# The low parts of the feed-forward weight units made by VectorE in place of GpSimd

## The chip, the cores and the metric

One Trainium2 chip, one of its cores. The metric is the device time of one execution in microseconds (us). Before the change it is 3954.25 us, the median of 3 runs (3954.13 to 3955.24). Lower is better.

## The reference, cut to what matters

Two model blocks run one after the other, on 512 tokens of width 1024. The first has two layers (a gated linear attention, a state space scan, memory attention); the change doesn't touch it. The second puts 16 meta tokens ahead of the 512 and has two layers, each a mixer and then a feed-forward block:

```
D_MODEL = 1024; D_FF = 4 * D_MODEL; N_META = 16; DEPTH = 2

def sq_relu_mlp(h, w1, w2):
    return jnp.square(jax.nn.relu(h @ w1)) @ w2

for i in range(DEPTH):
    g = norm_g[i]
    hn = rmsnorm(h, g[0])
    m = rwkv_pool_mixer(hn, ...) if i % 2 == 0 else diff_attn_mixer(hn, ...)
    h = h + rmsnorm(m, g[1])
    f = sq_relu_mlp(rmsnorm(h, g[2]), mlp_w1[i], mlp_w2[i])
    h = h + rmsnorm(f, g[3])
return h[:, N_META:]
```

## The kernel before, in words

**Weights.** All weights are one stream of units of 128 x 1024 floats. SyncE loads unit u into slot u mod 4 of `ring` (L2696 to L2709) once TensorE has begun unit u-2. The products of the feed-forward blocks are made at better than single-pass precision: a value is written as a high part, rounded to the format that TensorE takes in one pass, and a low part, the rest. For a unit of weights, ScalarE copies `ring` into one of two `high` buffers (`make_high`, L306 to L311), and GpSimd writes `ring` minus `high` into `ring_r` (`make_low`, L299 to L304) and counts the semaphore `unit_lo` up. TensorE waits for `unit_lo` before the first matmul of a unit (L184), and then issues for each of eight 128-row pieces k of the unit three products: high by high (L225), high weights by low activations (L228), low weights by high activations (L230). `make_high` of unit u+1 waits until TensorE has begun unit u (L310), so the parts are made one unit ahead.

**A feed-forward block** (`mlp`, L2590 to L2640) is four products, each a `Gemm`: in0, out0, in1, out1. An in-product makes 16 tiles of 128 features, from one unit each (8 k-pieces). An out-product makes 8 tiles from two units each. So there are 32 + 32 units in a block and 128 in both. In the first block (layer 0) a tile is 528 tokens wide, in two halves of 264; in the second (layer 1) 512. The f tiles of in0 are used up by out0, those of in1 by out1, which adds out0's sum.

**The engines' order.** Every engine runs the stages of the list `stages` in order, and within one its own loop; nothing is reordered on an engine, so a wait holds what stands behind it. Around a block:

- `Rms` (L399) norms the block's input. Its DVE part (L497 to L519) takes the reciprocal of the root (L505), and then for eight tiles k writes the normed tile (L513) and, two tiles later, the tile's low part `h_r` (L518), after ScalarE's high part `h_hi` (L478). Each of the eight low parts counts a semaphore.
- `rms.feed(g)` (L524 to L527) ties the first tile of in0 to these: `high` of its first unit is made in `Rms.scalar` (L475), before the normed tiles are there, and TensorE waits in the first tile for the low part of each k alone (L221, L222), not for all eight.
- ScalarE evacuates each in-tile with a relu (L2605). DVE's stage `Squares` (L2610 to L2627) then squares the tile (L2623), copies its high part `f_hi` (L2625) and makes its low part `f_r` (L2627).
- An out-product needs all 16 tiles' parts (L2638, L2639): TensorE and ScalarE wait for the last `f_r`. Its tiles are evacuated by ScalarE and VectorE in turn in out0 (L2243, L2246), by VectorE alone in out1 (L2608), whose squares for the next norm ScalarE makes (L441).
- The first matmul of any product waits until all tiles of the one before are evacuated (L201 to L203).

The core of the norm's DVE loop, for the order in which DVE's work stands:

```
507        for k in range(self.n + 2):
512            if k < self.n:
513                b.nc.vector.scalar_tensor_tensor(
514                    out=self.out(k), in0=self.view(self.x(k)), scalar=self.w(k),
516            if self.hi and k >= 2:
517                dve.wait_ge(b.out_hi, at["parts"] + k - 1)
518                b.nc.vector.tensor_tensor(self.lo(k - 2), self.out(k - 2), self.hi(k - 2),
```

Of the kernel before, what the change touches and what calls it, by code (L numbers as in the profile page):

```python
# [50 lines left out]
class Chain:  # L51


    def __init__(self, eng, sem):
        self.eng, self.sem, self.n = eng, sem, 0
# [29 lines left out]
class Stage:  # L85
# [8 lines left out]
    def vector(self, dve):  # L94
        pass

    def gpsimd(self, pool):
        pass


class Gemm(Stage):
# [13 lines left out]
    def __init__(self, b, name, kind, x, kt, outs, ranges, store, engines, needs, tiles=None, before=None,  # L115
                 high=None, x_hi=None, after=None, ready=None):
        self.ready = ready
        self.fed = False
        self.squared_by = None
        self.beside = False  # L120
        self.after = after
        self.b, self.name, self.kind, self.x, self.kt = b, name, kind, x, kt
        self.ranges, self.store, self.engines, self.needs = ranges, store, engines, needs
        self.tiles, self.before = tiles, before
        if kind == "fm":
            self.per_out = kt // 8
            self.slots = 4 if len(ranges) == 1 else 2
            self.body_outs = self.slots
            while self.body_outs * self.per_out % RING:
                self.body_outs += self.slots  # L130
            if outs < self.body_outs or outs % self.body_outs:
                self.body_outs = outs
            self.body_units = self.body_outs * self.per_out
            self.iters = outs // self.body_outs
            self.pars = [o % 2 for o in range(self.body_outs)]
        else:
            self.body_units = kt // 2
            self.body_outs = len(tiles)
            self.slots = len(tiles)
            self.iters = outs  # L140
            self.pars = [i % 2 for i in range(len(tiles))]
        self.unit0 = b.units
        self.full0 = list(b.full)
        self.body_par = [self.pars.count(0), self.pars.count(1)]
        self.peel = min(self.full0) == 0 or self.iters == 1 or before is not None or high is not None
        self.high, self.x_hi, self.split0 = high, x_hi, b.splits
        if high is not None:
            assert self.body_units % 2 == 0, name
            b.splits += self.body_units * self.iters
        b.units += self.body_units * self.iters  # L150
        b.full = [f + self.iters * n for f, n in zip(b.full, self.body_par)]
        self.done = list(b.full)
        if self.iters > 1:
            assert self.body_units % RING == 0, name
# [141 lines left out]
                it, j = divmod(u + 1, self.body_units)  # L296
                self.make_low(pool, j, it)

    def make_low(self, pool, j, it):  # L299

        b, slot = self.b, (self.unit0 + j) % RING
        pool.wait_ge(b.unit_hi, self.split0 + j + 1 + it * self.body_units)
        b.nc.gpsimd.tensor_tensor(b.ring_r[:, slot, :], b.ring[:, slot, :], self.high[:, j % 2, :],  # L303
                                  ALU.subtract).then_inc(b.unit_lo, 1)  # L304

    def make_high(self, act, j, it):  # L306
# [77 lines left out]
        evacuate(last, self.iters - 1, False)  # L384

    def gpsimd(self, pool):
        if self.high is None or self.beside:
            return

        def body(it):  # L390
            for j in range(self.body_units):
                self.make_low(pool, j, it)
        self.loop(pool, body)

    def vector(self, dve):
        self.evacuate(dve, "dve")


class Rms(Stage):  # L399
# [1757 lines left out]
def build(nc, a, out):  # L2157

    with ExitStack() as ctx:
        b = Board(nc, ctx)  # L2160
# [70 lines left out]
        def view(off, *shape):  # L2231
            n = int(np.prod(shape))
            ap = arena[:, off:off + n]
            if len(shape) == 1:
                return ap
            names = "abc"[:len(shape)]
            return ap.rearrange(f"p ({' '.join(names)}) -> p {' '.join(names)}",
                                **{c: s for c, s in zip(names[1:], shape[1:])})
# [89 lines left out]
        g = stages[-1]  # L2328
# [25 lines left out]
        g = stages[-1]  # L2354
# [10 lines left out]
        g = stages[-1]  # L2365
# [29 lines left out]
        g = stages[-1]  # L2395
# [24 lines left out]
        g = stages[-1]  # L2420
# [42 lines left out]
        g = stages[-1]  # L2463
# [61 lines left out]
        def norm_g(layer, i):  # L2525
            return lambda k: b.col("norm_g_2", (4 * layer + i) * 8 + k)
# [7 lines left out]
        def post(layer, i, g, kept=False):  # L2534

            if kept:
                rms = Rms(b, h3, KD, FULL, D, EPS, norm_g(layer, i), h3, [0], [], done(g), onto=x1, each=g.tile,
                          added=True)
            else:
                rms = Rms(b, h2, KD, HALVES, D, EPS, norm_g(layer, i), h2, [0, 1], [], done(g), onto=x2, each=g.tile,  # L2540
                          added=True)
            rms.follow(g)
            stages.append(rms)
            return rms
# [6 lines left out]
        def pre(layer, i, before, kept=False):  # L2551
            if kept:
                rms = Rms(b, x1, KD, FULL, D, EPS, norm_g(layer, i), h3, [2], [], hi=h3_hi, lo=h3_lo, each=before.tile)
            else:
                rms = Rms(b, x2, KD, HALVES, D, EPS, norm_g(layer, i), h2, [2, 3], [], hi=h_hi, lo=h2_lo,
                          each=before.tile)
            stages.append(rms)
            return rms
# [6 lines left out]
        def keep3(to):  # L2565
            return lambda which, m, parts, o: copy(which, to(m), parts[0])
# [23 lines left out]
        def mlp(layer, rms, kept=False):  # L2590

            at = META if kept else 0
            ranges = FULL if kept else HALVES
            f, f_lo, f_hi = b.f, b.f_lo, b.f_hi
            first = view(2 * F_TILES * L2, KD, L2)
            rms = pre(layer, 2, rms, kept)

            def filled(o, parts):
                return parts[0] if kept else b.ps[:, 2 * (o % 2):2 * (o % 2) + 2, 0:L2 // 2]

            def shaped(ap):
                return ap[:, at:] if kept else ap.rearrange("p (r t) -> p r t", r=2)

            def relu(which, m, parts, o):
                return nc.scalar.activation(shaped(f[:, m, :]), filled(o, parts), ACT.Relu)  # L2605

            def both_halves(which, m, parts, o):
                return nc.vector.tensor_tensor(shaped(b.h[:, m, :]), shaped(first[:, m, :]), filled(o, parts), ALU.add)  # L2608

            class Squares(Stage):  # L2610


                def __init__(self, g, base):
                    self.g, self.base = g, base

                def vector(self, dve):
                    with dve.Fori(0, 4) as it:
                        for o in range(4):
                            par, n = self.g.count(o, it)
                            done = it * 12 + (self.base + 3 * o)  # L2620
                            dve.wait_ge(b.stored[par], n)
                            t, hi, lo = (z[:, it * 4 + o, at:] for z in (f, f_hi, f_lo))
                            nc.vector.tensor_tensor(t, t, t, ALU.mult).then_inc(mlp_parts, 1)  # L2623
                            dve.wait_ge(mlp_parts, done + 1)
                            nc.vector.tensor_copy(hi, t).then_inc(mlp_parts, 1)  # L2625
                            dve.wait_ge(mlp_parts, done + 2)
                            nc.vector.tensor_tensor(lo, t, hi, ALU.subtract).then_inc(mlp_parts, 1)  # L2627

            for half in range(2):
                base = 48 * (2 * layer + half)  # L2630
                g = gemm(f"mlp{layer}_in{half}", h3_lo if kept else h2_lo, KD, 16, relu, A, [rms.ready], high,
                         h3_hi if kept else h_hi, ranges)
                if half == 0:
                    rms.feed(g)
                stages.append(Squares(g, base))
                whole = keep3(lambda m: first[:, m, META:]) if kept else keep2(lambda m: first[:, m, :])
                store, engines = (both_halves, V) if half else (whole, BOTH)
                g2 = gemm(f"mlp{layer}_out{half}", lambda k: f_lo[:, k, at:], 16, KD, store, engines,  # L2638
                          [(mlp_parts, base + 48)], high, lambda k: f_hi[:, k, at:], ranges)  # L2639
            return post(layer, 3, g2, kept)  # L2640

        rms = mlp(0, rms)


# [38 lines left out]
        for h in range(8):  # L2683
            o = lambda k, h=h: m3.o[:, h, :]
# [86 lines left out]
```

## Time and profile before

| | before |
|---|---|
| median of 3 runs | 3954.25 us (3954.13 to 3955.24) |
| the profiled execution's own time | 3962.14 us |
| its span | 3960.6 us |
| mean granted clock of TensorE | 0.879 |
| TensorE matmul busy | 3284.0 us, 83% |
| VectorE (DVE) busy | 1408.0 us, 36% |
| GpSimd (POOL) busy | 992.2 us, 25% |
| ScalarE (ACT) busy | 852.8 us, 22% |

The profile is of one execution. Its own time lies 7.9 us above the median of the runs without a profile. The span is from its first to its last instruction. The engine names in its rows are PE (TensorE's matmuls), PEld (its weight loads), DVE, ACT, POOL and SP (SyncE); L and a number is a line of the kernel. The granted clock is 1.0 where TensorE is given its 2.4 GHz and 0.5 at 1.2 GHz. An average over the whole span mixes stages with different limits, so what a change in one stage is worth has to be read in that stage. The first feed-forward block fills about 2557 to 2950 us of the span, the second about 3560 to 3940 us.

### The profile page before, as it was taken

What the parts mean: (1) busy time and instruction counts of PE and PEld (TensorE: products, weight loads), DVE (VectorE), ACT (ScalarE), POOL (GpSimd) and SP (SyncE); (2) the same over time, 40 slices, a digit from 0 to 9 for tenths busy, and PEclk for the clock granted to TensorE, in tenths of its full rate; (3) what the DMA queues carried; (4) which work ended last, traced back from release to release, by engine and by line L of the source; (5) the groups of instructions that cost most, each with busy time, mean ns of one, the idle gap of its engine ahead of it and who ended that gap; (6) DMA issues with size and microseconds to landing.
All of it is one profiled execution on the core that took longest, in us unless ns stands there. A gap on an engine that the chain in (4) does not pass through costs nothing.

```text
span 3960.6 us, 42750 instructions
## 1 busy us (share of the span) xinstructions
PE 3284.0 (83%) x16346; PEld 2473.8 (62%) x16346; DVE 1408.0 (36%) x2281; ACT 852.8 (22%) x1405; POOL 992.2 (25%) x691
## 2 busy tenths in 40 slices
PE   7997976698579699998895886899998855579997
PEld 4444745486466477446694775699988633337776
DVE  4663023501017512003326644350522243546052
ACT  2112222122012222001224111222222122222221
POOL 0220400243122276004340000043433400004443
PEclk9998976799879799999997996899999955589999
DMA  5991200023862168222220000122222100012222
GB/s 160 258 259 55 92 25 0 22 96 104 153 219 97 53 187 233 75 76 72 79 86 6 1 1 6 48 85 86 85 75 82 54 0 0 0 48 82 93 85 80
DMA packets 113984, 328.66 MB, mean 83 GB/s; under 512 B 35744, under 2 KB 36384, under 8 KB 113456
## 3 DMA queue, kind: packets, MB, share of 16 engines
q1 hardware_dynamic: 59040, 212.89, 16.9%
q0 software_dynamic: 32592, 101.46, 9.7%
q10 hardware_dynamic: 22208, 12.26, 1.2%
q8 instruction: 106, 1.74, 0.2%
q14 instruction: 38, 0.31, 0.0%
HBM read 290.48 MB, written 36.04 MB: 82 GB/s over the span
## 4 chain that ended last, share of the span: by engine, by line
PE 65%; DVE 18%; issue 5%; DMA 5%; POOL 4%; ACT 3%; DVEq 0%; ACTq 0%; POOLq 0%
PE ps L225 12%; PE ps L228 11%; PE ps L230 11%; PE ps L235 9%; DMA arena<-d_q 3%; DVE inv L505 2%; POOL ring_r L303 2%; PE ps L1918 2%; DVE h L513 2%; PE ps L1947 1%; PE ps L493 1%; PE ps L251 1%; PE ps L255 1%; DMA arena<-d_pb 1%; PE ps L254 1%
## 5 line engine op out<-in xcount | busy, mean ns | idle before, releaser
L303 POOL TENSOR_TENSOR ring_r<-ring,high 128x1024 fp32r<-128x1024 f32 x290 | 738.2, 2546 | 2107.2 <-ACT high L311 2106.8
L225 PE MATMUL ps<-h_hi,high 128*128 128x264 f32 (+1 forms) x1760 | 569.4, 335 | 73.7 <-DVE h_r L518 41.1
L228 PE MATMUL ps<-h_r,high 128*128 128x264 f32 (+1 forms) x1760 | 563.9, 332 | 0.0
L230 PE MATMUL ps<-h_hi,ring_r 128*128 128x264 f32 (+1 forms) x1760 | 496.8, 331 | 0.0
L311 ACT ACTIVATE high<-ring 128x1024 fp32r<-128x1024 f32 x290 | 305.9, 1055 | 601.3 <-PE ps L225 408.2
L225 PEld LDWEIGHTS ps<-h_hi,high 128*128 128x128 f32 x1760 | 336.5, 191 | 118.6 <-issue 71.3
L228 PEld LDWEIGHTS ps<-h_r,high 128*128 128x128 f32 x1760 | 337.9, 192 | 29.3
L235 PE MATMUL ps<-arena,ring 128*128 128x512 f32 (+1 forms) x896 | 337.5, 540 | 22.5 <-DVE arena L1759 10.0
L230 PEld LDWEIGHTS ps<-h_hi,ring_r 128*128 128x128 f32 x1760 | 300.8, 191 | 31.3
L235 PEld LDWEIGHTS ps<-arena,ring 128*128 128x128 f32 x896 | 172.5, 193 | 186.7 <-issue 158.6
L225 PE MATMUL ps<-f_hi,high 128*128 128x264 f32 (+1 forms) x768 | 241.3, 327 | 25.7 <-POOL ring_r L303 25.7
L228 PE MATMUL ps<-f_r,high 128*128 128x264 f32 (+1 forms) x768 | 239.9, 325 | 0.0
L235 PE MATMUL ps<-h,ring 128*128 128x512 f32 x512 | 220.3, 592 | 2.3 <-ACT arena L2243 2.3
L2246 DVE COPY arena<-ps 128x512 f32<-128x512 f32 (+4 forms) x32 | 21.2, 662 | 559.9 <-PE ps L230 284.5
L230 PE MATMUL ps<-f_hi,ring_r 128*128 128x264 f32 (+1 forms) x768 | 207.9, 325 | 0.0
L225 PE MATMUL ps<-z_hi,high 128*128 128x512 f32 x384 | 158.3, 412 | 37.3 <-POOL ring_r L303 36.3
L235 PEld LDWEIGHTS ps<-h,ring 128*128 128x128 f32 x512 | 97.1, 190 | 125.5 <-issue 125.5
L225 PEld LDWEIGHTS ps<-f_hi,high 128*128 128x128 f32 x768 | 147.8, 192 | 38.5 <-issue 26.9
L2627 DVE TENSOR_TENSOR f_r<-f,f_hi x64 | 157.4, 2460 | 2.2
L2243 ACT ACTIVATE arena<-ps 128x512 f32<-128x512 f32 (+6 forms) x104 | 59.7, 576 | 451.4 <-PE ps L230 256.4
L228 PE MATMUL ps<-z_lo,high 128*128 128x512 f32 x384 | 156.1, 407 | 0.0
L228 PEld LDWEIGHTS ps<-f_r,high 128*128 128x128 f32 x768 | 148.0, 193 | 11.7
(381 smaller groups left out, 4879.4 us busy)
## 6 DMA issues: line engine op xcount, KB each, us to landing
ring<-in_units SPq DMA_DIRECT2D x402, 512.0 KB, 3.5
d_ca<-arena POOLq DMA_DIRECT2D x16, 640.0 KB, 5.9
arena<-d_ca POOLq DMA_DIRECT2D x16, 640.0 KB, 5.0
arena<-in_s_bk POOLq DMA_DIRECT2D x16, 512.0 KB, 9.5
arena<-d_q POOLq DMA_DIRECT2D x32, 256.0 KB, 12.0
d_pb<-arena POOLq DMA_DIRECT2D x16, 512.0 KB, 7.2
arena<-d_pb POOLq DMA_DIRECT2D x16, 512.0 KB, 6.0
arena<-d_ca POOLq DMA_DIRECT2D x16, 512.0 KB, 6.7
```

The source lines that it names most:

```text
L225: part = mm(acc, hi[:, cols], self.x_hi(k)[:, t0:t0 + tn], start=(k == 0), stop=False)
L228: mm(acc, hi[:, cols], self.x(k)[:, t0:t0 + tn], start=False, stop=False)
L230: ins = mm(acc, w[:, cols], self.x_hi(k)[:, t0:t0 + tn], start=False, stop=(k == self.kt - 1))
L235: ins = mm(acc, w[:, k % 8 * P:(k % 8 + 1) * P], self.x(k)[:, t0:t0 + tn], start=(k == 0), stop=(k == self.kt - 1))
L251: part = mm(out, self.x_hi(k)[:, tok], hi, start=(k == 0), stop=False)
L303: b.nc.gpsimd.tensor_tensor(b.ring_r[:, slot, :], b.ring[:, slot, :], self.high[:, j % 2, :], ALU.subtract).then_inc(b.unit_lo, 1)
L311: b.nc.scalar.activation(self.high[:, j % 2, :], b.ring[:, u % RING, :], ACT.Copy).then_inc(b.unit_hi, 1)
L505: b.nc.vector.reciprocal(b.inv[:, 0:self.tokens], b.root[:, 0:self.tokens]).then_inc(b.inverted, 1)
L513: b.nc.vector.scalar_tensor_tensor(out=self.out(k), in0=self.view(self.x(k)), scalar=self.w(k), in1=self.view(b.inv[:, 0:self.tokens]), op ...
L1918: ins = mm(b.ps[0:nt, 2 * (n % 2) + c, 0:min(nk, 512)], q, k[:, 0:min(nk, 512)], start=True, stop=True)
L2243: return nc.scalar.activation(to, ps, ACT.Copy, scale=1.0 if scale is None else scale)
L2627: nc.vector.tensor_tensor(lo, t, hi, ALU.subtract).then_inc(mlp_parts, 1)
```

## The change

In both feed-forward blocks, and there alone, `make_low` is issued on VectorE. GpSimd has no instruction left in these eight products. In the in-products the stage `Squares` makes unit 0's low part first, and then, for each tile o, the low part of unit o+1 ahead of the squaring of tile o. Its loop of four passes over four tiles is written out. In the out-products `Gemm.vector` does the same around the evacuations that are VectorE's.

```
+        self.low_by = "pool"
...
+    def low_unit(self, dve, u):
+
+        if u < self.body_units * self.iters:
+            it, j = divmod(u, self.body_units)
+            self.make_low(dve, j, it)
+
+    def make_low(self, eng, j, it):
...
-        pool.wait_ge(b.unit_hi, self.split0 + j + 1 + it * self.body_units)
-        b.nc.gpsimd.tensor_tensor(b.ring_r[:, slot, :], b.ring[:, slot, :], self.high[:, j % 2, :],
+        eng.wait_ge(b.unit_hi, self.split0 + j + 1 + it * self.body_units)
+        which = b.nc.gpsimd if self.low_by == "pool" else b.nc.vector
+        which.tensor_tensor(b.ring_r[:, slot, :], b.ring[:, slot, :], self.high[:, j % 2, :],
                                   ALU.subtract).then_inc(b.unit_lo, 1)
...
     def gpsimd(self, pool):
-        if self.high is None or self.beside:
+        if self.high is None or self.beside or self.low_by != "pool":
             return
...
     def vector(self, dve):
-        self.evacuate(dve, "dve")
+        if self.low_by != "dve":
+            self.evacuate(dve, "dve")
+            return
+        b = self.b
+        self.low_unit(dve, 0)
+        for m in range(self.body_outs * self.iters):
+            for u in range(m * self.per_out + 1, (m + 1) * self.per_out + 1):
+                self.low_unit(dve, u)
+            it, o = divmod(m, self.body_outs)
+            if self.engines[self.pars[o]] == "dve":
+                par, n = self.count(o, it)
+                dve.wait_ge(b.filled[par], n)
+                self.store("dve", m, self.bank(o), o).then_inc(b.stored[par], 1)
+                if self.squared_by and m >= 2:
+                    self.squared_by.add(dve, m - 1)
...
                 def vector(self, dve):
-                    with dve.Fori(0, 4) as it:
+                    self.g.low_unit(dve, 0)
+                    for it in range(4):
                         for o in range(4):
+                            self.g.low_unit(dve, it * 4 + o + 1)
                             par, n = self.g.count(o, it)
...
+                g.low_by = "dve in Squares"
                 stages.append(Squares(g, base))
...
+                g2.low_by = "dve"
```

Lines of the changed kernel are 22 to 24 higher than those above: its L311 is L303, L540 is L518, L535 is L513, L2647, L2649 and L2651 are L2623, L2625 and L2627, and L2268 is L2246. Two places show the new order.

VectorE (DVE) at the start of in0 of layer 0, before: the last rows of the norm, then the first passes of `Squares`. `h_r` is the low part of a normed tile, `out_hi` the semaphore of its high part.

```order
L513 SCALAR_TENSOR_TENSOR h<-x,cols,inv 128x528
L518 TENSOR_TENSOR h_r<-h,h_hi 128x528 [waits out_hi] x3
L2617 UNCONDITIONAL_BRANCH
L2617 ISA
L2623 ISA [waits stored_even]
L2623 TENSOR_TENSOR f<-f 128x528
```

The same place in the changed kernel:

```order
L535 SCALAR_TENSOR_TENSOR h<-x,cols,inv 128x528
L540 TENSOR_TENSOR h_r<-h,h_hi 128x528 [waits out_hi] x3
L311 TENSOR_TENSOR ring_r<-ring,high 128x1024 [waits unit_hi] x2
L2647 TENSOR_TENSOR f<-f 128x528 [waits stored_even]
L2649 CAST f_hi<-f 128x528 [waits mlp_parts]
L2651 TENSOR_TENSOR f_r<-f,f_hi 128x528 [waits mlp_parts]
L311 TENSOR_TENSOR ring_r<-ring,high 128x1024 [waits unit_hi]
L2647 TENSOR_TENSOR f<-f 128x528 [waits stored_odd]
```

The low parts of units 0 and 1 now stand on VectorE behind the last low part of the norm; before, GpSimd had nothing else in its queue at this place.

VectorE from the last evacuations of out0 into in1 of layer 0, in the changed kernel (before, the rows of L2246 and of `Squares` stood here alone):

```order
L2268 COPY arena<-ps 128x528 [waits filled_odd]
L311 TENSOR_TENSOR ring_r<-ring,high 128x1024 [waits unit_hi] x3
L2268 COPY arena<-ps 128x528 [waits filled_odd]
L311 TENSOR_TENSOR ring_r<-ring,high 128x1024 [waits unit_hi] x2
L2647 TENSOR_TENSOR f<-f 128x528 [waits stored_even]
```

The low part of in1's first unit is the first of the two behind the last evacuation.

## Rows read from the trace of the kernel before

**Rows 1.** The page, part 1: busy us, share of the span, instructions.
```profile
PE 3284.0 (83%) x16346; PEld 2473.8 (62%) x16346; DVE 1408.0 (36%) x2281; ACT 852.8 (22%) x1405; POOL 992.2 (25%) x691
```
**Rows 2.** The page, part 4: the chain that ended last, by line.
```profile
PE ps L225 12%; PE ps L228 11%; PE ps L230 11%; PE ps L235 9%; DMA arena<-d_q 3%; DVE inv L505 2%; POOL ring_r L303 2%; PE ps L1918 2%; DVE h L513 2%; PE ps L1947 1%; PE ps L493 1%; PE ps L251 1%; PE ps L255 1%; DMA arena<-d_pb 1%; PE ps L254 1%
```
**Rows 3.** Timeline, layer 0's in0 begins: start us, us, instruction [idle before <-releaser].
```profile
2551.99 2.34 POOL L303 TENSOR_TENSOR ring_r<-ring,high 128x1024 fp32r<-128x1024 f32 x1 [123.55 <-ACT high L311]
2557.44 0.56 PE L225 MATMUL ps<-h_hi,high 128*128 128x264 f32 x1 [7.36 <-DVE h_r L518]
2563.08 1.94 DVE L518 TENSOR_TENSOR h_r<-h,h_hi 128x528 fp32r<-128x528 f32 x3
2567.31 0.39 PE L225 MATMUL ps<-h_hi,high 128*128 128x264 f32 x1 [1.02 <-POOL ring_r L303]
```
**Rows 4.** Timeline at the beginning of layer 1's in0.
```profile
3566.23 1.89 DVE L518 TENSOR_TENSOR h_r<-h,h_hi 128x512 fp32r<-128x512 f32 x3
3570.43 0.50 PE L225 MATMUL ps<-h_hi,high 128*128 128x512 f32 x1 [1.11 <-POOL ring_r L303]
```
**Rows 5.** Groups by line on DVE: count | busy us, mean ns | idle.
```profile
L1663 DVE TENSOR_TENSOR arena<-ps,memn 128x1024 f32<-128x1024 f32 x8 | 9.8, 1225 | 15.0 <-PE ps L1575 15.0
```
**Rows 6.** Timeline at three of the four in-to-out places, with two second units.
```profile
2658.11 1.06 ACT L311 ACTIVATE high<-ring 128x1024 fp32r<-128x1024 f32 x1 [2.20 <-DVE f_r L2627]
2659.25 2.34 POOL L303 TENSOR_TENSOR ring_r<-ring,high 128x1024 fp32r<-128x1024 f32 x1 [11.24 <-ACT high L311]
2661.73 0.56 PE L225 MATMUL ps<-f_hi,high 128*128 128x264 f32 x1 [6.46 <-POOL ring_r L303]
2670.49 1.06 ACT L311 ACTIVATE high<-ring 128x1024 fp32r<-128x1024 f32 x1 [7.04 <-PE ps L225]
...
2859.44 0.56 PE L225 MATMUL ps<-f_hi,high 128*128 128x264 f32 x1 [6.46 <-POOL ring_r L303]
...
3660.52 0.77 PE L225 MATMUL ps<-f_hi,high 128*128 128x512 f32 x1 [6.41 <-POOL ring_r L303]
3668.20 1.06 ACT L311 ACTIVATE high<-ring 128x1024 fp32r<-128x1024 f32 x1 [5.76 <-PE ps L225]
```
**Rows 7.** Timeline: steady tiles of in0, layer 0 and layer 1.
```profile
2602.79 0.61 ACT L2605 ACTIVATE f<-ps 128x528 f32 x1 [4.29 <-PE ps L230]
2603.56 0.71 DVE L2623 TENSOR_TENSOR f<-f  x1 [1.75 <-ACT f L2605]
2604.43 2.65 POOL L303 TENSOR_TENSOR ring_r<-ring,high 128x1024 fp32r<-128x1024 f32 x1 [3.19 <-ACT high L311]
2604.86 2.79 DVE L2627 TENSOR_TENSOR f_r<-f,f_hi  x1
2608.64 0.61 ACT L2605 ACTIVATE f<-ps 128x528 f32 x1 [4.29 <-PE ps L230]
...
3576.30 0.60 ACT L2605 ACTIVATE f<-ps 128x512 f32<-128x512 f32 x1 [4.21 <-PE ps L230]
3577.08 0.69 DVE L2623 TENSOR_TENSOR f<-f  x1 [4.87 <-ACT f L2605]
3581.86 0.60 ACT L2605 ACTIVATE f<-ps 128x512 f32<-128x512 f32 x1 [4.01 <-PE ps L230]
```
**Rows 8.** Timeline: the f_r of in0's second-last tile, layer 0.
```profile
2651.63 0.71 DVE L2627 TENSOR_TENSOR f_r<-f,f_hi  x1
```
**Rows 9.** Timeline from out0 to in1 of layer 0.
```profile
2758.25 0.71 DVE L2246 COPY arena<-ps 128x528 f32 x1 [22.69 <-PE ps L230]
2759.21 0.36 PE L225 MATMUL ps<-h_hi,high 128*128 128x264 f32 x1 [1.14 <-DVE arena L2246]
```
**Rows 10.** Windows: length; busy of PE, PEld, DVE, ACT, POOL; granted clock; DMA.
```profile
2655.50:2660.00 4.50, 0.00 (x0) 0.00 (x0) 1.85 (x3) 1.47 (x2) 0.75 (x1) 1.00 0.00 0
2855.00:2859.40 4.40, 0.00 (x0) 0.00 (x0) 0.76 (x2) 1.06 (x1) 2.34 (x1) 0.50 0.00 0
3533.40:3535.40 2.00, 0.00 (x0) 0.00 (x0) 0.69 (x1) 1.13 (x2) 0.00 (x0) 1.00 0.00 0
```

More of the change, by code:

```diff
@@ L297, in out_gpsimd @@
                 self.make_low(pool, j, it)
-    def make_low(self, pool, j, it):
+    def low_unit(self, dve, u):
[3 more added lines that the diff above has]
+    def make_low(self, eng, j, it):
         b, slot = self.b, (self.unit0 + j) % RING
-        pool.wait_ge(b.unit_hi, self.split0 + j + 1 + it * self.body_units)
-        b.nc.gpsimd.tensor_tensor(b.ring_r[:, slot, :], b.ring[:, slot, :], self.high[:, j % 2, :],
+        eng.wait_ge(b.unit_hi, self.split0 + j + 1 + it * self.body_units)
+        which = b.nc.gpsimd if self.low_by == "pool" else b.nc.vector
+        which.tensor_tensor(b.ring_r[:, slot, :], b.ring[:, slot, :], self.high[:, j % 2, :],
                                   ALU.subtract).then_inc(b.unit_lo, 1)
```

## The prediction

> **What bounds the kernel now.** The page's busy shares come first [rows 1]: TensorE is busy for 83% of the span, VectorE for 36%, GpSimd for 25%. The chain that ended last [rows 2] says the same by line: the split products L225, L228 and L230 lead it, and GpSimd's low part L303 has 2%. So of GpSimd's work only what lies in a gap of TensorE can be on the path, and the question goes to the timelines of the two feed-forward blocks. Three kinds of place are there.
>
> In a steady tile TensorE never waits. In layer 0 one relu starts at 2602.79 and the next at 2608.64 [rows 7], so a unit takes 5.85 us; in layer 1 it is 3576.30 to 3581.86, 5.56 us. GpSimd's 2.65 us lie inside. What GpSimd does to VectorE there is visible too: f_r takes 2.79 us while a GpSimd low part runs [rows 7] and 0.71 us where none does [rows 8].
>
> Where an in-product ends and an out-product begins, TensorE stands still for 6.46 us, released by GpSimd [rows 6]: squares, `high` at 2658.11, low part at 2659.25 for 2.34 us, first matmul at 2661.73. There are four such places, two in each layer.
>
> Where a norm feeds in0, GpSimd makes the first low part at 2551.99, long before it is wanted. TensorE begins the tile at 2557.44, released by the first `h_r`, and works beside the norm's remaining seven [rows 3]. The last of these ends at 2563.08 + 1.94 = 2565.02, and unit 1 begins at 2567.31. Layer 1 is alike: 3568.12 and 3570.43 [rows 4].
>
> **What the change does, part by part.** The changed price is that of one low part on VectorE. No row has this form. The nearest is a VectorE subtraction or product over the same 128x1024 elements with one operand in PSUM, 1.225 us [rows 5]; f_r, scaled from 528 elements and its 0.71 us to 1024, would give at most 1.38. I take 1.22, since its row has the same number of elements. GpSimd's 2.34 is the other end; at that price nothing would be gained where a low part is exposed.
>
> *In to out, four times.* The last squares, `high`, the low part and the first matmul still follow one another. 2.34 becomes 1.22, a gain of 1.12 each: **-4.5 us**. At 1.38 it is -3.8.
>
> *Start of in0, twice.* The order of VectorE's work has the first low part behind all eight `h_r`, and TensorE waits for it before its first matmul. The tile that ran beside the norm now starts after it. Layer 0: 2565.02 + 1.22 + 0.14 (0.14 is what passed from the end of the low part at 2661.59 to the matmul at 2661.73 [rows 6]) = 2566.4. The tile then takes a warm 5.85 us and what the clock costs. TensorE's first matmul takes 0.56 us after the norm and 0.39 us ten microseconds later [rows 3], so it starts on the lower clock. What a whole unit pays for that is seen after the in-to-out gap: 2661.73 to the next unit's `high` at 2670.49 is 8.76 us, less about 0.07 of latency and 5.85, so 2.85 more; in layer 1, 3660.52 to 3668.20, less 0.07 and 5.56, 2.05 more [rows 6]. I take 2.5, between the two, for either layer. Unit 1 can then begin at 2566.4 + 5.85 + 2.5 = 2574.7, where it began at 2567.31: 7.4 us later. Its own low part is ready by then, since `high` follows the first matmul at once and has the whole tile. Layer 1: 3568.12 + 1.36 + 5.56 + 2.5 = 3577.5 for 3570.43, 7.1 us. Together **+14.5 us**. If the clock cost nothing it would be +9.5, with 2.85 in both +15.2.
>
> *Out0 to in1, twice.* The evacuation of out0's last tile starts at 2758.25 and ends at 2758.96, and TensorE starts at 2759.21, released by it [rows 9]. The low part was ready; now it stands behind this evacuation on VectorE: +1.22 each, **+2.4 us**. TensorE's gap grows from 1.14 to 2.36 us.
>
> *The steady tiles, at nothing.* For tile o VectorE does the low part of unit o+1 and then tile o's squares, and what can be late is the low part that stands behind these squares. Layer 0: f_r starts at 2604.86 and, with GpSimd idle, ends at 2605.57 [rows 7, 8]; low part until 2606.8, TensorE released at 2606.9, wanted at about 2608.4, just ahead of the next relu. Spare: 1.5 us. Layer 1: squares from 3577.08, f_r 1.30 later as in layer 0, low part done at 3577.08 + 1.30 + 0.69 + 1.22 = 3580.3, released at 3580.4, wanted at 3581.6. Spare: 1.2 us. In the out-products VectorE's only other work is an evacuation or a sum of 0.7 us every second unit. `high` is still made one unit ahead and waits for nothing of VectorE's. The same holds for the DMA queue of SyncE, which waits for TensorE alone; GpSimd's queue only loses instructions. The loop written out costs VectorE no time that TensorE sees with over 1 us of spare.
>
> Here a rule bears. The Trainium skill (SBUF — State Buffer, Who interferes with whom) says that a VectorE instruction with two SBUF inputs and a GpSimd one that reads SBUF take turns on a shared read port, and that the loser stands still for the other's whole length. The rows agree: f_r ends 0.57 us after GpSimd's low part (2607.65 and 2607.08). By the rule f_r is short once GpSimd has left, which is what rows 8 show already; without it f_r could stay long, and that is the third rival.
>
> Another rule speaks for the change. The Trainium skill (GPSIMD Engine Reference, Engine selection) puts two-input elementwise work on VectorE, GpSimd being about twice as slow. The rows agree on the factor (2.34 against 1.225), but counted for all 128 low parts it would be 143 us, of which the sum above lets the path see 4.5.
>
> **Sum.** -4.5 + 14.5 + 2.4 = +12.4 us. On the profiled execution's own 3962.14 us that is 3974.5; that execution lies 7.9 us above the median of the runs, and the same difference on the median, 3954.25, gives **3966.7 us**.
>
> **Rivals.**
>
> *The clock stays up from in to out (the other side: not slower).* TensorE's gap there shrinks from 6.46 to 5.3 us. If the granted clock no longer fell in it, each of the four out-products would save the 2.5 us of its first unit as well: 12.4 - 10 = +2.4, 3956.6 us. It decides on whether the fall comes later than 5.3 us after the last matmul. For it: in the first of these gaps the clock is still full until 2660.00 [rows 10], 4.7 us after the last matmul (2661.73 - 6.46 = 2655.27 [rows 6]). Against: in the second of them, which begins at 2859.44 - 6.46 = 2852.98 [rows 6], it is at half from 2855.00 on [rows 10], and it has to stay up four times. Chance 0.08.
>
> *The clock falls before in1.* The gap of 2.36 us is longer than the 2.0 us without a matmul from 3533.40 to 3535.40, through which the clock stayed full [rows 10], and longer than the 2.0 us after which it had fallen in the gap just named. If it falls in both layers, 2 x 2.5: +17.4, 3971.7 us; in one, 3969.2. Chance 0.15.
>
> *VectorE becomes the bound of the in-products.* If f_r stayed at 2.79 us, or the low part took over 2.4, the low part would come late in each steady tile: in layer 0 2604.86 + 2.79 + 1.36 = 2609.0 for 2608.4, 0.6 us; in layer 1 0.9 us by the same count. 30 tiles of each, +45: 4012 us. Rows 8 speak against it. Chance 0.02.
>
> That it comes out faster for a reason that I don't see has 0.03. The forecast keeps 0.72.
>
> **How the numbers follow.** About 0.2%, 7.9 us, is what a measurement of this kernel can tell from no change: above 3962.2 is slower, below 3946.3 faster. The forecast's own range is 3962 to 3970 (from the in0 starts at almost no clock cost to the upper ends of all terms); it lies above the bound but for its low end, and so do the second rival and the third. I count 0.1 of the forecast's 0.72 as within the bound: slower 0.62 + 0.15 + 0.02 = 0.79, same 0.08 + 0.1 = 0.18, faster 0.03. The range, 3958 to 3973, reaches down to halfway to the first rival and up over the second with both layers and a low part at 1.38.
>
> **What would show it.** Right: at in0 in the changed profile TensorE idles for some 16 us with its first L225 released by the low part on DVE, about 1.4 us after the last `h_r`; relu to relu stays 5.85 and 5.56 us; the four in-to-out gaps are about 5.3 us; the gap before in1 is 2.3 to 2.4 us; f_r takes 0.7 us in all tiles; the low part on DVE takes 1.22 us. Wrong: waits of TensorE on the low part inside an in-product, a first unit of an out-product that starts with matmuls at the full clock, a low part much longer than 1.22 us, or a first tile of in0 that still overlaps the norm.

## The result, and the profile after

The change makes the kernel slower by a little: 3959.95 us, the median of 17 runs (3949.74 to 3971.6), against 3951.06 us for the kernel before (17 runs, 3937.59 to 3960.89). The ratio is 1.0027 with a 95% interval of 1.0014 to 1.0039, so +10.7 us, between +5.5 and +15.4; the two medians lie 8.9 us apart. The forecast was +12.4 us, and 3966.7 us on a median of before that more runs put 3.2 us lower (3951.06 for 3954.25).

The page of the kernel after, part 1, answers to [rows 1]:

```profile
span 3958.4 us, 42302 instructions
PE 3276.7 (83%) x16346; PEld 2470.5 (62%) x16346; DVE 1438.9 (36%) x2409; ACT 852.7 (22%) x1405; POOL 673.0 (17%) x563
```

and these are the two groups of the low part, of part 5 (count | busy us, mean ns | idle before):

```profile
L311 POOL TENSOR_TENSOR ring_r<-ring,high 128x1024 fp32r<-128x1024 f32 x162 | 417.4, 2577 | 1147.2 <-ACT high L319 1147.1
L311 DVE TENSOR_TENSOR ring_r<-ring,high 128x1024 fp32r<-128x1024 f32 x128 | 156.5, 1223 | 195.9 <-ACT high L319 195.9
```

128 low parts went from GpSimd to VectorE at 1.223 us each. GpSimd lost 319 us of work, VectorE gained 31 (157 for the low parts, less what f_r no longer loses). Neither number is in the kernel's time.

The profiled span of after is 2.2 us *shorter* than that of before, although the runs say slower. A pair of profiles doesn't settle a difference of this size as a whole; it does when read stage by stage. These are the reciprocals (L505 before, L527 after) ahead of in0 and behind out1, in the timelines of VectorE. Before:

```profile
2551.06 3.45 DVE L505 RECIPROCAL inv<-root 128x528 f32<-128x528 f32 x1 [2.86 <-ACT root L472]
2960.28 3.45 DVE L505 RECIPROCAL inv<-root 128x528 f32<-128x528 f32 x1 [2.20 <-ACT root L472]
...
3943.13 3.35 DVE L505 RECIPROCAL inv<-root 128x512 f32<-128x512 f32 x1 [2.00 <-ACT root L472]
```

After:

```profile
2542.49 3.45 DVE L527 RECIPROCAL inv<-root 128x528 f32<-128x528 f32 x1 [2.86 <-ACT root L494]
2956.49 3.45 DVE L527 RECIPROCAL inv<-root 128x528 f32<-128x528 f32 x1 [2.20 <-ACT root L494]
...
3548.57 3.35 DVE L527 RECIPROCAL inv<-root 128x512 f32<-128x512 f32 x1 [2.65 <-ACT root L494]
...
3941.36 3.35 DVE L527 RECIPROCAL inv<-root 128x512 f32<-128x512 f32 x1 [2.00 <-ACT root L494]
```

The stages ahead of the first block, which the change doesn't touch, took 8.57 us less in this execution, those between the blocks 2.2 less. The block of layer 0 went from 409.22 to 414.00 us, that of layer 1 from 388.60 (its reciprocal before started at 3554.53) to 392.79: **+8.97 us** in the two. This count, from reciprocal to reciprocal, is used for all runs below. From run to run it still holds the chance of how the granted clock falls and comes back around TensorE's gaps. In the six kernels here that have an in-to-out gap of 5.0 to 5.1 us, one execution of each, the first units of the four out-products (from the first matmul to the third `high`) add up to 30.9 to 34.4 us. So some 3 us between two kernels can be this alone, and smaller differences are read by place.

Where the 8.97 us come from, by places. The start of layer 0's in0, which answers to [rows 3] (timelines of VectorE and TensorE, after):

```profile
2554.51 1.94 DVE L540 TENSOR_TENSOR h_r<-h,h_hi 128x528 fp32r<-128x528 f32 x3
2556.37 1.22 DVE L311 TENSOR_TENSOR ring_r<-ring,high 128x1024 fp32r<-128x1024 f32 x1
2557.88 0.56 PE L226 MATMUL ps<-h_hi,high 128*128 128x264 f32 x1 [16.36 <-DVE ring_r L311]
```

TensorE stands idle for 16.36 us where it stood for 7.36, and its first matmul is released by the low part behind the last `h_r`. From in to out, and from out0 to in1, which answer to [rows 6] and [rows 9]:

```profile
2657.71 1.23 DVE L311 TENSOR_TENSOR ring_r<-ring,high 128x1024 fp32r<-128x1024 f32 x1 [1.12 <-ACT high L319]
2659.09 0.56 PE L226 MATMUL ps<-f_hi,high 128*128 128x264 f32 x1 [5.09 <-DVE ring_r L311]
2666.72 1.06 ACT L319 ACTIVATE high<-ring 128x1024 fp32r<-128x1024 f32 x1 [5.92 <-PE ps L226]
...
2754.34 0.71 DVE L2268 COPY arena<-ps 128x528 f32<-128x528 f32 x1 [8.78 <-PE ps L231]
2754.96 1.22 DVE L311 TENSOR_TENSOR ring_r<-ring,high 128x1024 fp32r<-128x1024 f32 x1
2756.32 0.36 PE L226 MATMUL ps<-h_hi,high 128*128 128x264 f32 x1 [2.02 <-DVE ring_r L311]
```

| place | before | after | measured | forecast |
|---|---|---|---|---|
| in0, layer 0: reciprocal to tile 1's relu | 22.40 | 29.69 | +7.29 | +7.4 |
| in0, layer 1: the same | 21.77 | 27.76 | +5.99 | +7.1 |
| in to out, the four gaps | 6.46, 6.46, 6.41, 6.42 | 5.09, 5.09, 5.04, 5.04 | -5.5 | -4.5 |
| the four first units of the out-products, from the first matmul to the third `high` | 8.76, 8.88, 7.68, 7.86 | 7.63, 7.84, 7.59, 7.87 | -2.3 | 0 |
| out0 to in1, the two gaps | 1.14, 0.99 | 2.02, 2.00 | +1.9 | +2.4 |
| in1's first unit, layer 0, to its relu | 6.11 | 7.63 | +1.5 | 0 |
| sum | | | +8.9 | +12.4 |

The steady tiles did not change: relu follows relu after 5.85 us in layer 0 and 5.55 to 5.56 us in layer 1, before and after.

### The profile page after: what moved, and what is told of

Read it like the earlier page. It is cut to its first block, busy times and chain, and to the rows that moved or that the text cites. A ratio compares the mean times of both kernels' runs of the same rounds, so it can differ in the third digit from the quotient of the medians.

```text
span 3958.4 us, 42302 instructions
## 1 busy us (share of the span) xinstructions
PE 3276.7 (83%) x16346; PEld 2470.5 (62%) x16346; DVE 1438.9 (36%) x2409; ACT 852.7 (22%) x1405; POOL 673.0 (17%) x563
## 4 chain that ended last, share of the span: by engine, by line
PE 71%; DVE 16%; POOL 4%; issue 4%; ACT 3%; DMA 2%; ACTq 0%; DVEq 0%; POOLq 0%
PE ps L236 15%; PE ps L226 11%; PE ps L229 11%; PE ps L231 11%; DVE inv L527 2%; POOL ring_r L311 2%; PE ps L1940 2%; DVE h L535 2%; DMA arena<-d_pb 1%; PE ps L1969 1%; PE ps L515 1%; POOL arena L1213 1%; PE ps L252 1%; PE ps L256 1%; PE ps L255 1%
## 5 line engine op out<-in xcount | busy, mean ns | idle before, releaser
L311 POOL TENSOR_TENSOR ring_r<-ring,high 128x1024 fp32r<-128x1024 f32 x162 | 417.4, 2577 | 1147.2 <-ACT high L319 1147.1
L311 DVE TENSOR_TENSOR ring_r<-ring,high 128x1024 fp32r<-128x1024 f32 x128 | 156.5, 1223 | 195.9 <-ACT high L319 195.9
L2268 DVE COPY arena<-ps 128x512 f32<-128x512 f32 (+3 forms) x32 | 21.2, 662 | 406.8 <-PE ps L236 138.1
## 6 DMA issues: line engine op xcount, KB each, us to landing
arena<-d_q POOLq DMA_DIRECT2D x32, 256.0 KB, 11.4
```

The lines of the kernel that those rows point to most:

```text
L311: which.tensor_tensor(b.ring_r[:, slot, :], b.ring[:, slot, :], self.high[:, j % 2, :], ALU.subtract).then_inc(b.unit_lo, 1)
```

## The experiments

In these runs the sum of the two blocks is counted as above, from one profiled execution of each kernel: 797.8 us before, 806.8 after the change.

Theory: the loss is the overlap of in0's first tile with the norm, taken away because the first low part stands behind the norm's work on VectorE; the gain is a shorter low part in the four exposed chains; the steady tiles are indifferent. Rival: VectorE's extra work costs time in the steady tiles, or the written-out loops do.

**Only the four first low parts of the in-products back on GpSimd.**

```
-        if u < self.body_units * self.iters:
+        if u < self.body_units * self.iters and self.on_dve(u):
...
-        if self.high is None or self.beside or self.low_by != "pool":
+        if self.high is None or self.beside:
+            return
+        if self.low_by != "pool":
+            for u in range(self.body_units * self.iters):
+                if not self.on_dve(u):
+                    it, j = divmod(u, self.body_units)
+                    self.make_low(pool, j, it)
             return
...
                 g.low_by = "dve in Squares"
+                g.on_dve = lambda u: u > 0
```

> The changed kernel, but the low part of unit 0 of each of the four in-products is made by GpSimd again; the other 124 low parts stay on VectorE. Each block is counted from the reciprocal ahead of in0 to the reciprocal behind out1: before 409.22 us (layer 0) and 388.60 us (layer 1), after the change 414.00 and 392.79, together +8.97. Theory (the loss is the place of the first low part in VectorE's order): both in0 starts get their overlap with the norm back and the gap before in1 is 1.1 us again, so only the in-to-out gain is left. Together 4.5 to 5.5 us below before, plus or minus what the granted clock does at four starts (up to 3 us); the whole kernel some 15 us under the changed one. Rival (VectorE's low parts cost time in the steady tiles, or the written-out loops do): both blocks stay within 3 us of the changed kernel's.

The blocks took 404.22 and 386.06 us, 7.5 us under before and 16.5 under the change. The kernel's ratio to before is 0.9977 (0.9961 to 0.9992). TensorE begins beside the norm again, and the gap before in1 of layer 1 is back (timeline of TensorE):

```profile
2554.70 0.56 PE L227 MATMUL ps<-h_hi,high 128*128 128x264 f32 x1 [7.36 <-DVE h_r L547]
...
3741.43 0.47 PE L227 MATMUL ps<-h_hi,high 128*128 128x512 f32 x1 [0.99 <-DVE arena L2275]
```

So four instructions out of 128 carried the whole loss. The gain is larger than expected by some 2 us, and the timeline has them. In both kernels unit 0 of in0 runs beside the norm, and its tile's relu and the next stand 7.13 us apart before and 6.03 us in this run (6.94 and 5.80 in layer 1). Before, TensorE waits 1.02 us for the low part of unit 1 ([rows 3]); on VectorE it is ready in time. That wait had been in the rows, and the forecast did not ask what would become of it.

**The complement: only these four on VectorE.** (The same edit with `g.on_dve = lambda u: u == 0`, and the out-products' low parts on GpSimd.)

> The complement: the low part of unit 0 of each in-product alone on VectorE, the other 124 on GpSimd as before. Theory: the whole loss without the gain, in0's starts 7.3 us later each, in1's gap 0.9 us longer each, in-to-out gaps 6.46 us as before: both blocks together 14 to 18 us above before. Rival (steady tiles): less than 5 us above before.

415.31 and 396.16 us, together 13.7 over before; ratio 1.0031 (1.0017 to 1.0044). That is 0.3 us below the lower end of the 14 to 18 expected, and far from the rival's 5. The in-to-out gaps are 6.25 and 6.20 us, not 6.46: `Squares` is written out here as well, and with it the square's chain is 0.2 us shorter (from the relu to the end of f_r 2.56 us for 2.77 at in0's last tile). This is what the forecast of 1.12 us a gap lacked: 6.46 to 6.25 is the loop, 6.25 to 5.09 the low part.

**Only the out-products on VectorE.** (The first experiment's edit with `g.on_dve = lambda u: False`.)

> VectorE makes the low parts of the out-products alone (64 units); those of the in-products are GpSimd's. Theory: the same times as with only the in-products' first units on GpSimd, 4.5 to 5.5 us below before for both blocks, in-to-out gaps of 5.1 us, since where the steady in-tiles' low parts are made is worth nothing. f_r takes 2.8 us again in the in-products. Rival (moving the steady in-tiles to VectorE is worth something, for or against): the two differ by more than 3 us that the granted clock does not account for.

405.38 and 388.30 us, 4.1 under before, with gaps of 5.09 and 5.04 us; ratio 0.9969 (0.9948 to 0.999). The difference to the first experiment is 3.4 us, where none was expected. 2.2 of it is the low part of unit 1 described there (here the relus are 7.14 us apart again), so it does matter at that one unit who makes it; another 0.9 us lies in the first units of the out-products, and the rest is too small to place. In the steady tiles f_r is long again, without any effect on TensorE (timeline of VectorE):

```profile
2604.97 0.43 DVE L2656 CAST f_hi<-f 128x528 fp32r<-128x528 f32 x1
2605.44 2.79 DVE L2658 TENSOR_TENSOR f_r<-f,f_hi 128x528 fp32r<-128x528 f32 x1
```

**The first low part on VectorE, but ahead of the norm's tiles.**

```
         b.nc.vector.reciprocal(...).then_inc(b.inverted, 1)
+        if self.low_first:
+            self.low_first.low_unit(dve, 0)
         dve.wait_ge(b.inverted, at["inverted"] + 1)
         for k in range(self.n + 2):
...
-                    self.g.low_unit(dve, 0)
+                    if self.base % 96:
+                        self.g.low_unit(dve, 0)
...
+                    rms.low_first = g
```

> The changed kernel with in0's first low part still on VectorE, but between the norm's reciprocal and its first normed tile. Theory (what costs is the overlap lost, not the engine): the norm is put back by 1.2 us, TensorE begins on the first h_r again and runs beside the norm; in0's unit 1 begins 1.2 to 2.5 us later than before instead of 7.3, and the two blocks together come out within 4 us of before. Rival (VectorE makes the first tile late wherever it stands): still 7 us above before.

405.98 and 388.89 us, 2.9 under before and 11.9 under the change; ratio 0.9985 (0.9972 to 0.9999). The timelines of VectorE and TensorE:

```profile
2534.89 1.16 DVE L311 TENSOR_TENSOR ring_r<-ring,high 128x1024 fp32r<-128x1024 f32 x1
2535.97 2.11 DVE L538 SCALAR_TENSOR_TENSOR h<-x,cols,inv 128x528 f32<-128x528 f32 x3
...
2538.85 0.56 PE L226 MATMUL ps<-h_hi,high 128*128 128x264 f32 x1 [8.30 <-DVE h_r L543]
```

The norm is put back by about 1 us and the overlap is whole. It is the place in the queue that costs, not the engine. Even the 1 us is earned back at unit 1, whose low part is now VectorE's: from the reciprocal to tile 1's relu it is 22.27 us, against 22.40 before. The expectation had unit 1 begin 1.2 to 2.5 us later than before.

**One and two more VectorE instructions in each steady in-tile.** (A subtraction of `high` from itself into an unused 128x1024 tile, 1.22 us, ahead of the low part; the result of the kernel doesn't use it. Each of the two kernels was executed once, 3946.95 and 3992.61 us, so only its blocks are compared.)

> The changed kernel with one more VectorE instruction of the low part's form (128x1024, 1.22 us, into an unused tile) ahead of the low part in each steady tile of the in-products, 15 x 4. Theory (spare of 1.5 us in layer 0, 1.2 us in layer 1): layer 0's relu-to-relu stays 5.85 us, layer 1's 5.56 us or at most 0.1 us more; the blocks are 0 to 4 us above the changed kernel's 414.00 and 392.79. Rival (VectorE's work in these tiles is on the path): +1.2 us a tile, 73 us.

> Two such instructions more. Theory: the spare is used up: a tile is late by about 2.45 less 1.5 = 1.0 us in layer 0 and 2.45 less 1.2 = 1.3 us in layer 1, so layer 0's block grows by about 30 us and layer 1's by about 38 us over the changed kernel's. Rival (VectorE is never waited for there): no change. Second rival (it was on the path all along): 2.45 us a tile, 147 us.

With one more: 413.95 and 395.11 us, 2.3 over the change, the relus in layer 1 still 5.55 us apart. All of the 2.3 lies in layer 1 outside the steady tiles, 1.3 in the first tile of in0 and 1.0 in the first units of the out-products. The spare is there. With two more: 422.91 and 406.29, +8.9 and +13.5 us, where 30 and 38 were expected. TensorE is late now, but not in every tile (timeline of TensorE, then ScalarE, layer 0):

```profile
2581.30 0.36 PE L227 MATMUL ps<-h_hi,high 128*128 128x264 f32 x1 [0.31 <-DVE ring_r L312]
2593.45 0.39 PE L227 MATMUL ps<-h_hi,high 128*128 128x264 f32 x1 [0.22 <-DVE ring_r L312]
```

```profile
2587.43 0.61 ACT L2634 ACTIVATE f<-ps 128x528 f32<-128x528 f32 x1 [4.60 <-PE ps L232]
...
2593.38 0.61 ACT L2634 ACTIVATE f<-ps 128x528 f32 x1 [4.39 <-PE ps L232]
...
2599.74 0.61 ACT L2634 ACTIVATE f<-ps 128x528 f32 x1 [4.80 <-PE ps L232]
...
2605.64 0.61 ACT L2634 ACTIVATE f<-ps 128x528 f32 x1 [4.34 <-PE ps L232]
```

The relus come after 5.95, 6.36 and 5.90 us: the waits are two tiles apart. The low part of unit u+1 hangs on the end of unit u-1 (relu, squares, extra work, low part), that is, one unit back from the wait. A chain that is too long by some amount delays unit u+1 by it, but the unit after it then starts its own chain from an end that was not late, and meets its time. So two units together lose the amount once. (In in1 of layer 0 it is shared out between the two, with 6.07 and 6.23 us from relu to relu; the pair comes to the same 12.3.) Between the first and the last relu of the four in-products the tiles take 8.3 us more than in the changed kernel in layer 0 and 11.4 in layer 1, with 14 such pairs in each: 0.59 and 0.82 us a pair. The rest of the 8.9 and 13.5 lies at the starts and the ends. The expectation counted the amount in every tile, as the third rival of the forecast did, which is twice too often. The spare itself was off as well: with 2.45 us of extra work the 0.59 and 0.82 leave 1.9 and 1.6 us, where the forecast had 1.5 and 1.2; of the 0.4 the shorter, written-out square chain is 0.2.

**What in-to-out is made of.** The kernel before, with all low parts on GpSimd, and one other edit: `high` of an out-product's first unit is made before the last relu, not behind the last squares.

```
         self.loop(act, body)
+        if self.next:
+            self.next.make_high(act, 0, 0)
         evacuate(last, self.iters - 1, False)
...
+                g.next, g2.fed = g2, True
```

> The kernel before with one other edit: ScalarE makes the high part of an out-product's first unit before it evacuates the in-product's last tile, not after the last squares; all low parts stay on GpSimd. Theory (at in-to-out the low part is only one of three pieces that stand in a row, and the chain high-low does not depend on the squares): the four gaps fall from 6.46 us to about 2.9 us (relu 0.7, squares 2.0, latency), 3.5 us each, 14 us in all, three times what the change gains there; and where the granted clock stays up through the shorter gap a first unit saves up to 2.5 us more, so the blocks come out 12 to 24 us below before. Rival (the low part on VectorE is what shortens the gap, something else holds TensorE): less than 5 us below before.

398.51 and 382.07 us, 17.2 under before; ratio 0.9937 (0.9916 to 0.9958). The gaps are 2.86 and 2.82 us, released by the last f_r (timeline of TensorE):

```profile
2656.58 0.39 PE L226 MATMUL ps<-f_hi,high 128*128 128x264 f32 x1 [2.86 <-DVE f_r L2630]
```

The theory holds: both parts of the unit's split stood behind the squares for no reason in the data, and taking them out is worth 3.6 us a place where the faster low part was worth 1.16.

**What is left of it.** The last wait is for the last squares, and only the first tile's last k-piece needs those.

```
-                g.next, g2.fed = g2, True
+                g.next, g2.fed, g2.needs = g2, True, []
+                g2.ready = lambda k, base=base: (mlp_parts, base + 3 * k + 3)
```

> The kernel before (all low parts on GpSimd) with the earlier high part of the run with the high part handed over, and with TensorE waiting in an out-product's first tile for each f tile's parts alone instead of for all 16. Theory (what is left at in-to-out is the wait for the last squares): the four gaps fall from 6.46 us (2.86 with the hand-over alone) to about 1.1 us, the size of the gap from out0 to in1, and the granted clock stays up: the two blocks together 26 to 34 us below before's 797.8. Rival (the gap is filled by another wait, such as the evacuation or the last squares of unit 1): no better than the hand-over's 780.6.

393.38 and 373.77 us, 30.7 under before; ratio 0.993 (0.9913 to 0.9946), median 3918.77 us. The gap is 0.75 us in layer 0 and 0.73 in layer 1, less than the 1.1 expected, and the clock stays full. Of the 31 us, 22.8 are the gaps themselves; the four first units, at full clock from their first matmul on, take 8.3 us less than before. In layer 0 (timeline of TensorE, and windows: length; busy of PE, PEld, DVE, ACT, POOL; granted clock; DMA):

```profile
2647.20 0.36 PE L226 MATMUL ps<-f_hi,high 128*128 128x264 f32 x1 [0.75 <-issue]
```

```profile
2646.00:2647.20 1.20, 0.45 (x5) 0.28 (x3) 0.00 (x0) 0.61 (x1) 0.00 (x0) 1.00 0.00 0
2647.20:2653.00 5.80, 5.80 (x48) 5.80 (x49) 1.85 (x3) 1.07 (x1) 2.73 (x1) 1.00 0.27 90
```

**The same two edits with the low parts on VectorE** (120 of the 128; the eight first units on GpSimd).

> The same two edits on the changed kernel, with only unit 0 of each of the eight products on GpSimd and the other 120 low parts on VectorE. Theory (a low part that is hidden costs the same on either engine): within 2 us of the same edits with all low parts on GpSimd, but for the granted clock. Rival (VectorE's shorter low part is still worth its 1.1 us at some place): at least 4 us below it.

392.55 and 372.68 us, 32.6 under before and 1.9 under the run with GpSimd; ratio 0.9914 (0.9896 to 0.9932), median 3918.48 us. The medians of the two are 0.3 us apart and the intervals of their ratios overlap. The 1.9 us lie where a GpSimd low part is still exposed, at unit 1 of in0: from the reciprocal to tile 1's relu it is 21.34 and 20.64 us here, 22.41 and 21.77 with GpSimd, 2.2 us together. Everywhere else the low part is hidden, and the engine that makes it does not matter measurably. Both versions beat the kernel before by 0.7% and 0.9%, and the change by about 1%.

## Why the prediction was right, point by point

*What bounds the kernel.* Right. Moving 319 us of GpSimd's work changed the time only at the eight places where TensorE stood still.

*The price of a low part, 1.22 us from a row of the same size.* Measured 1.223.

*In to out.* The mechanism was right and the term small by 1 us: 1.16 us a gap for the low part, and 0.2 for the written-out square loop, which the forecast had at no cost and no gain. The first units of the out-products took 2.3 us less in this execution, 2.2 of it in layer 0 (7.63 and 7.84 us). That is this execution's luck as far as the runs show: in the six kernels with the same gap these two units took 7.55 to 8.91 us each.

*The start of in0.* Right in mechanism and place. Layer 0 +7.29 for 7.4. Layer 1 +5.99 for 7.1: the first tile paid 1.4 us for the lower clock (from first matmul to relu 7.22 us against 5.83 at full clock) and not 2.5. The 2.5 was a middle of 2.05 and 2.85; 1.4 lies outside both. Two things are in this. Both ends were read 0.4 us (layer 0) and 0.5 us (layer 1) too high: the same stretch, first matmul to third `high`, takes 6.30 and 6.13 us where the clock stays full (the kernel with both edits at in-to-out), and not the 5.92 and 5.63 that the forecast took off, so the rows had shown a price of 2.5 and 1.55 us. And the price changes from execution to execution: the first tile of layer 1's in0, from its first matmul to its relu, took 7.22 us in the change, but 8.52 in its complement and 8.50 with one more instruction, behind the same gap of 15.8 us.

*Out0 to in1.* +0.9 and +1.0 for 1.22. VectorE starts the low part 0.1 us before the evacuation ends, and in layer 0 the gap behind out0's written-out loop is 0.14 us shorter to begin with (1.00 for 1.14 us in the first experiment; in layer 1 0.99 for 0.99).

*The steady tiles at nothing.* Shown: unchanged intervals, and one whole extra low part in each in-tile still fits.

*The rule on the shared read port.* The Trainium skill (SBUF — State Buffer, Who interferes with whom) says that a VectorE instruction with two SBUF inputs contends with a GpSimd instruction that reads SBUF. The traces agree from both sides: f_r takes 0.71 us (0.69 in layer 1) in every tile of after, and 2.77 to 2.80 us again in 54 of 64 tiles of the run that leaves the in-products on GpSimd.

*The rivals.* The first, that the clock stays up from in to out, did not happen: the first matmul after each of the four gaps of after takes 0.56 or 0.76 us. The third did not happen, and by the run with two more instructions its price was more than twice too high. The second happened in one of the two layers, in a form the forecast had not thought of (last section), at 1.5 us instead of 2.5.

*The size.* The forecast of +12.4 lies inside the interval of 5.5 to 15.4. The ledger's +8.97 is one execution's, with 2.3 us of clock in its favour and 1.5 against it. The median of after, 3959.95 us, is 6.75 below the 3966.7 forecast: inside the stated range of 3958 to 3973, outside the narrower 3962 to 3970 given with it, and just below 3962.2, from which the forecast would have called it slower. 3.2 of the 6.75 are the median of before, which came out lower; the other 3.5 are the terms, 1 of them in-to-out. The first units of the out-products and of in1, both at nothing in the forecast, moved by -2.3 and +1.5 us; that these two nearly cancel is luck.

## What to carry to other kernels

When work is moved to a faster engine, ask first what stands ahead of its *first* instance on the new queue; 124 of 128 moved instructions were harmless or good, and four, of which two landed behind a norm and two behind an evacuation, turned 7 us of gain into 9 of loss. Where a gap is a chain of steps, look for steps that are in it by program order alone, or by a wait for more than the first piece needs: taking these out gained 31 us, 8 of them by the clock that then stayed up, and making one step twice as fast 5.

## What the runs showed of the hardware that was not expected

TensorE's granted clock can fall after TensorE has gone back to work. The gap of 2.02 us before in1 of layer 0 was passed at full clock, matmuls ran at it for over a microsecond, and then it fell (windows of after, columns as above):

```profile
2754.50:2756.20 1.70, 0.00 (x0) 0.00 (x0) 1.68 (x2) 0.00 (x0) 0.00 (x0) 1.00 0.00 0
2756.40:2757.50 1.10, 1.10 (x10) 1.10 (x11) 0.00 (x0) 0.72 (x1) 0.00 (x0) 1.00 0.00 0
2758.00:2761.00 3.00, 3.00 (x15) 3.00 (x15) 1.10 (x1) 0.00 (x0) 0.00 (x0) 0.50 0.45 164
2761.50:2763.90 2.40, 2.40 (x22) 2.40 (x22) 0.00 (x0) 0.00 (x0) 0.00 (x0) 1.00 0.00 0
```

Five kernels of this study (the change, its complement, the first low part ahead of the norm, one and two more instructions) have this gap of 2.0 to 2.2 us, each in both layers, in one execution. In three of these ten places the first unit took 1.5 to 1.6 us more than in the others; in the rest the clock stayed up. After the 2.8 us gaps of the hand-over it was three of four: from the first matmul to the third `high` 7.84 and 6.32 us in layer 0 and 7.73 and 7.71 in layer 1, where the run without the gap took 6.30 and 6.13, though the first matmul ran at full clock in all four. So the duration of the first matmul after a gap doesn't tell whether the gap costs clock; the length of the whole unit does.
